# Half of the depthwise convolution's taps on VectorE instead of TensorE, in a two-layer decoder step

## The reference, cut to what matters

```python
def conformer_conv(h, buf, w_pw1, b_pw1, w_dw, b_dw, ln_g, ln_b, w_pw2):
    u = h @ w_pw1 + b_pw1
    u = u[..., :D_CONV] * jax.nn.sigmoid(u[..., D_CONV:])
    full = jnp.concatenate([buf.astype(u.dtype), u], axis=1)
    z = lax.conv_general_dilated(full, w_dw[:, None, :], (1,), 'VALID', ..., feature_group_count=D_CONV) + b_dw
    z = jax.nn.silu(layernorm(z, ln_g, ln_b))
    return z @ w_pw2, full[:, -(CONV_WIDTH - 1):]
```

## Time and profile before

| | us |
|---|---|
| median of 3 runs | 823.9 |
| lowest and highest | 823.81, 825.25 |
| the profiled execution's own time | 823.19 |
| its span, first to last instruction | 821.6 |
| TensorE busy | 749.0 (91%) |
| VectorE busy | 322.2 (39%) |
| ScalarE busy | 208.4 (25%) |
| mean granted TensorE clock | 0.968 |

### The profile page before, as it was taken

The page is one execution under the profiler, slowest core; times in us unless marked ns, Lnnn a source line. Parts: engine busy times, 40 slices in busy tenths (PEclk is TensorE's granted clock), DMA queues, the critical chain, the costliest instruction groups (busy, mean ns, idle before and its releaser), DMA issues.

```text
span 821.6 us, 16618 instructions
## 1 busy us (share of the span) xinstructions
PE 749.0 (91%) x6420; PEld 532.6 (65%) x6420; DVE 322.2 (39%) x952; ACT 208.4 (25%) x498; POOL 59.0 (7%) x101
## 2 busy tenths in 40 slices
PE   8999999999979879889999898999999798788894
PEld 6877577766646446648876456777766465456483
DVE  3434343523323131334556656243233231313445
ACT  2100242521212111123225543143311111111232
POOL 1600200000000000000052620000000000000000
PEclk9999999999999898999999999999999899989998
DMA  9873896799999999999358774994999999999901
GB/s 358 301 257 85 246 420 250 277 407 424 421 418 424 421 419 422 414 412 397 138 191 300 242 208 177 421 408 173 419 419 421 420 420 420 421 419 416 375 2 53
DMA packets 65346, 271.83 MB, mean 331 GB/s; under 512 B 8032, under 2 KB 19504, under 8 KB 45296
## 3 DMA queue, kind: packets, MB, share of 16 engines
q1 hardware_dynamic: 58320, 260.30, 79.7%
q10 hardware_dynamic: 4048, 5.84, 2.3%
q0 software_dynamic: 2896, 4.58, 1.9%
HBM read 262.44 MB, written 3.61 MB: 324 GB/s over the span
## 4 chain that ended last, share of the span: by engine, by line
PE 52%; DMA 20%; SPq 5%; DVE 2%; ACT 2%; issue 2%; DVEq 0%; ACTq 0%
PE bank L630 17%; DMA ring<-in_moe_w_up 11%; PE bank L772 11%; PE bank L746 7%; DMA arena<-in_moe_w_up 6%; PE bank L801 4%; SPq L2236 3%; PE bank L815 3%; DMA ring<-in_moe_w_down 2%; DMA arena<-in_moe_w_down 2%; PE bank L1105 1%; PE bank L707 1%; PE bank L940 1%; SPq L2226 1%; PE bank L1130 1%
## 5 line engine op out<-in xcount | busy, mean ns | idle before, releaser
L772 PE MATMUL bank<-ring,arena 128*32 128x256 f32 x1344 | 115.5, 411 | 13.7 <-DMA ring<-in_moe_w_up 10.3
L630 PE MATMUL bank<-xn_sq,ring 128*128 128x264 f32 x480 | 108.6, 387 | 1.1 <-issue 0.6
L746 PEld LDWEIGHTS bank<-arena 128*128 128x128 f32 x864 | 99.0, 192 | 9.2 <-issue 9.1
L630 PE MATMUL bank<-arena,ring 128*128 128x264 f32 (+1 forms) x440 | 103.0, 389 | 0.1
L746 PE MATMUL bank<-arena 128*128 128x128 f32 (+1 forms) x864 | 102.6, 277 | 0.5 <-DVE arena L1419 0.5
L630 PEld LDWEIGHTS bank<-xn_sq,ring 128*128 128x128 f32 x480 | 90.8, 190 | 18.5 <-issue 2.3
L1451 DVE TENSOR_TENSOR arena<-arena,bank 128x128 f32<-128x128 f32 x34 | 9.8, 287 | 220.0 <-ACT arena L1900 220.0
L772 PEld LDWEIGHTS bank<-ring,arena 128*32 128x32 f32 x1344 | 61.4, 118 | 52.9 <-issue 30.2
L630 PEld LDWEIGHTS bank<-arena,ring 128*128 128x128 f32 x440 | 81.9, 190 | 18.3 <-issue 3.8
L772 PE MATMUL bank<-xn_sq,arena 128*32 128x256 f32 x384 | 52.9, 437 | 21.7 <-DMA ring<-in_moe_w_up 21.7
L1469 DVE TENSOR_TENSOR hT<-hT,bank 128x264 f32<-128x264 f32 x144 | 61.5, 428 | 20.6 <-PE bank L826 11.8
(11 more groups left out here) (278 smaller groups left out, 868.9 us busy)
## 6 DMA issues: line engine op xcount, KB each, us to landing
ring<-in_stream SPq DMA_DIRECT2D x34, 1024.0 KB, 12.6
ring<-in_moe_w_gate SPq DMA_DIRECT2D x34, 1024.0 KB, 19.3
ring<-in_moe_w_up SPq DMA_DIRECT2D x34, 1024.0 KB, 21.4
ring<-in_moe_w_down SPq DMA_DIRECT2D x28, 1024.0 KB, 21.9
arena<-in_moe_w_down SPq DMA_DIRECT2D x24, 1024.0 KB, 22.1
arena<-in_moe_w_gate SPq DMA_DIRECT2D x14, 1024.0 KB, 19.0
arena<-in_moe_w_up SPq DMA_DIRECT2D x14, 1024.0 KB, 21.1
xn_sq<-in_moe_w_gate SPq DMA_DIRECT2D x12, 1024.0 KB, 18.8
```

The source lines that it names most:

```text
L630: t = mm(ps[:, 0:cols], lhs(k), rhs(k), start=(k == 0), stop=(k == n - 1))
L746: t = mm(bank[k // 4][:, (k % 4) * n:(k % 4 + 1) * n], XR[:, i, k * P:(k + 1) * P], S[:, j % 2, i, 0:n], start=(i == 0), stop=(i == 2))
L772: t = mm(bank[2 + r][p0:p0 + U, 0:F].rearrange("p (c f) -> p c f", c=2), x, w[i][:, :, k * F + c * P:k * F + (c + 1) * P], start=(k == 0), ...
```

## The change

Chunks 0 to 3 (two pairs, `PD = 2`, `CD = 4`) leave TensorE's taps. VectorE computes them as 31 accumulating instructions for each chunk, 124 in all, on 128 partitions by 256 tokens, straight from `uT` at offset j. Two chunks alternate. Each instruction waits for the end of the one two before it (`s_tap`). From chunk 2 on, four of them stand between line 1263 and the wait for the sigmoid, and nine behind the gating: 13 in each of six chunks, 78 in all; the last 46 stand behind the loop. TensorE does only `taps(2)` and `taps(3)`, both behind `expand(7)`; `taps(0)` between `expand(4)` and `expand(5)` is gone. The copies for pairs 0 and 1 and half of the diagonals are gone too, the waits of pairs 2 and 3 for a free buffer with them. The tap weights `wdw` and `wq` move to another place of the arena, and `dg` is half as large.

```diff
+PD = 2
+CD = 2 * PD
+NTAPS = CD * CW
+TAPS_WAITING, TAPS_EACH = 4, 13
...
-            if p == 0:
+            if p == PD:
                 eng.wait_ge(s_zero, 2)
-            if p >= 2:
+            if p >= PD + 2:
                 arrive(eng, ("taps", 2 * (p - 2) + 1))
...
             for c in range(KD):
                 expand(c)
-                if c == 4:
-                    taps(0)
-            for p in range(1, PAIRS):
+            for p in range(PD, PAIRS):
                 taps(p)
...
                 v.tensor_tensor(sgu[:, c % 4, :], ps[:, 0:T], rstd[:], ALU.mult).then_inc(is_free(key), 1)
+                if c >= 2:
+                    vector_taps((c - 2) * TAPS_EACH, TAPS_WAITING)
                 dve.wait_ge(s_sgu, c + 1)
...
+            def vector_taps(start, n):
+
+                for i in range(start, min(start + n, NTAPS)):
+                    c, j = 2 * (i // (2 * CW)) + i % 2, i % (2 * CW) // 2
+                    src = uT[:, c, j:j + TP]
+                    if j == 0:
+                        dve.wait_ge(s_glu, c + 1)
+                        v.tensor_scalar(zT[:, c, 0:TP], src, tap[:, c, 0:1], vcol("conv_b_dw", c), ALU.mult, ALU.add)\
+                         .then_inc(s_tap, 1)
+                    else:
+                        dve.wait_ge(s_tap, i - 1)
+                        v.scalar_tensor_tensor(out=zT[:, c, 0:TP], in0=src, scalar=tap[:, c, j:j + 1],
+                                               in1=zT[:, c, 0:TP], op0=ALU.mult, op1=ALU.add).then_inc(s_tap, 1)
...
             for c in range(KD):
                 glu(c)
-                if c == 4:
-                    prompt_taps(0)
-                    prompt_taps(1)
-                    add_chunk(1)
+                if c >= 2:
+                    vector_taps((c - 2) * TAPS_EACH + TAPS_WAITING, TAPS_EACH - TAPS_WAITING)
...
-            for c in range(2, KD):
+            vector_taps((KD - 2) * TAPS_EACH, NTAPS)
+            dve.wait_ge(s_tap, NTAPS)
+            for c in range(1, CD):
+                add_chunk(c)
+            for c in range(CD, KD):
                 prompt_taps(c)
...
-                if c and c % 2 == 0:
+                if c > CD and c % 2 == 0:
                     shift(c // 2 - 1)
...
-            for c in range(KD):
-                g.tensor_tensor(dg[:, c], wq[:, c * NQ * TQ:(c + 1) * NQ * TQ].unsqueeze(2)
+            for c in range(CD, KD):
+                g.tensor_tensor(dg[:, c - CD], wq[:, c * NQ * TQ:(c + 1) * NQ * TQ].unsqueeze(2)
...
             for p in range(PAIRS):
-                shift_blocks(sp, "sp", p)
+                if p >= PD:
+                    shift_blocks(sp, "sp", p)
```

More of the change, by code:

```diff
@@ L270, in build @@
         mu, q = place(q, T)
-        dg, q = place(q, KD, NQ * TQ, CG)
+        wdw, q = place(q, CW * KD)
+        wq, q = place(q, KD * NQ * TQ)
+        dg, q = place(q, KD - CD, NQ * TQ, CG)
         shifted = []
@@ L275, in build @@
             shifted.append(u4)
-        wdw, q = place(q, CW * KD)
-        wq, q = place(q, KD * NQ * TQ)
         assert q <= ARENA, q
@@ L411, in build @@
         s_dve = sem("dve_steps")
-        s_pl = sem("pool_steps")
+        s_tap = sem("taps_on_vector")
         s_zc = sem("centred_chunks")
@@ L536, in copied @@
         def copied(eng, p):
-            eng.wait_ge(s_u4[p % 2], sum(by_queue(x) for x in range(p % 2, p + 1, 2)))
+            eng.wait_ge(s_u4[p % 2], sum(by_queue(x) for x in range(p % 2, p + 1, 2) if x >= PD))
             if copies("pool", p):
@@ L656, in taps @@
                     ps = open_bank(pe, ("taps", c))
-                    pe.wait_ge(s_dg, c + 1)
+                    pe.wait_ge(s_dg, c - CD + 1)
                     for q in range(TQ):
                         for b in range(NQ):
-                            t = mm(ps[CG * b:CG * (b + 1), 0:TP], dg[:, c, TQ * b + q, :],
+                            t = mm(ps[CG * b:CG * (b + 1), 0:TP], dg[:, c - CD, TQ * b + q, :],
                                    shifted[p % 2][:, b, c % 2, NQ * q:NQ * q + TP], start=(q == 0), stop=(q == TQ - 1))
@@ L1282, in add_chunk @@
             def add_chunk(k):
-                freed(dve, ("taps", k))
+                if k >= CD:
+                    freed(dve, ("taps", k))
                 if k > 1:
@@ L2106, in _ @@
             pool.dma_start(spill[:, 0:PIN_EARLY], early_pins).then_inc(s_spill[0], 16)
[L2107 to L2112, removed]
             def moe(l):
```

## The result

The changed kernel takes 829.02 us (the median of 20 executions, 824.26 to 833.82), the kernel before beside it on the same chip 822.86 us (20 executions, 819.25 to 830.1). The ratio is 1.0070, 95% interval 1.0053 to 1.0088: slower by some 6 us. The forecast was 831.3 us in a range of 826.5 to 842.

What follows compares the result with a forecast made beforehand. TensorE was taken to set the pace until 96 us, VectorE's taps after the change: 6.1 us later there plus 1.3 us of clock, +7.4 on 823.19, 830.6; with 0.7 for the median 831.3, range 826.5 to 842.

Steps and rivals of the forecast that it cites:

- Who sets the end: End of the tap stage: VectorE's taps finish last, and TensorE, done at 88.1 us, waits 14 us for them.
- The sum for VectorE: VectorE's gating, sample taps and 124 taps end at 98.1 us; after additions the last bias line starts 6.1 us later.
- The diagonals: GpSimd's diagonals beside VectorE's first gatings: with four instead of eight, gating runs clean and chunk 2 starts 2.6 us earlier.
- TensorE's taps: TensorE's conv taps: two pairs fewer save 14.2 us; after 6.6 us idle the last pair ends at 88.1.
- The clock: TensorE's two sums after its 14 us wait run at a lower clock: 0.9 plus 0.4, 1.3 us in all.
- Passed on one to one: Behind the stage everything keeps its order, so the delay of 6.1 + 1.3 = 7.4 us reaches the total.
- No overlap: Rival on VectorE's taps: each waits for the one before, 0.48 us each, +9.9 us, 841.2; chance 0.10.
- Cheap taps: Rival on VectorE's taps: 0.345 us each, like a tensor_tensor, VectorE ends 6.8 us earlier, 824.5; chance 0.06.
- a faster kernel: Rival on VectorE's taps: distance under 0.327 us gives a gain; at 0.30 the time is 819; chance 0.04.
- Swallowed later: Rival behind the stage: the weight stream swallows the delay, 824 us; chance 0.04.
- Starved copies: Rival on GpSimd's five copies of the last pair: starved beside VectorE's stream, +16 us, 840; chance 0.03.

Runs made afterwards that it cites:

- without the tail: The changed kernel with the last 46 of 124 taps not done; total of 1394.49 us says nothing, first subtraction at 91.48 us.
- with dearer taps: The changed kernel with taps chunk by chunk, each waiting for the one directly before; 840.86 us, ratio 1.0234.
- with another place for TensorE's wait: The changed kernel with eleven instead of 13 taps between gatings, so twelve taps move behind the loop; 829.01 us, ratio 1.0093.
- four extra diagonals: The changed kernel with GpSimd building four more unused diagonals ahead of the four needed; 833.97 us, ratio 1.0140.
- the repeat: The changed kernel timed again with no edit; 828.78 us, ratio 1.0089; its profiled execution took 823.42 us.
- with one pair: The changed kernel with PD = 1: VectorE keeps two chunks (62 taps), TensorE three pairs; 815.58 us, ratio 0.9917.
- the late wait: The changed kernel with VectorE's wait for tap weights and conv state moved to the first instruction touching the state; 827.19 us, ratio 1.0049.
- with idle products: Three kernels: the changed kernel plus unused TensorE products, 25 calls behind taps(3), or 12 ahead of it and 25 or 31 behind; ratios 1.0015, 1.0061, 1.0130.
- with three chunks: The changed kernel with chunk 3's taps back on TensorE (VectorE keeps 93) and the later state wait; 813.55 us, ratio 0.9883.
- the kernel with 25 calls of idle products: The changed kernel with 25 calls of unused TensorE products behind taps(3), ahead of the sum over channels; 824.58 us, ratio 1.0015.
- the kernel with the short filling: The kernel with three chunks on VectorE, plus the state's transfer issued by SP and four calls of idle products; 814.98 us, ratio 0.9904.

## Why the prediction was right

The forecast held in its sign, its range and its mechanism; its +7.4 us was a little high against some 6. The steps on the stage are shown one by one; what happens behind `w_pw2` agrees over medians only.

| step | forecast | profile after |
|---|---|---|
| distance of two taps | 0.40 | 0.396 |
| chunk 2 starts | 33.8 | 33.61 |
| last tap ends | 98.1 | 97.1 |
| TensorE's wait ahead of the last pair | 6.6 | 5.59 |
| TensorE's last pair ends | 88.1 | 88.6 |
| TensorE's wait for VectorE | 14 | 12.61 |
| last bias line, later by | 6.1 | 5.0 |
| clock, until the first subtraction | 0.9 | 1.07 |
| clock, sum of squares | 0.4 | 0 |
| `w_pw2`, later by | 7.4 | 6.05 |

- **Who sets the end.** Right, and shown from both sides: without the tail the stage is 12.35 us shorter, with dearer taps 14.4 us longer, with another place for TensorE's wait the same within 0.8 us.
- **The sum for VectorE.** It was 1.1 us too large. The last tap ends 1.0 earlier: 0.2 from the earlier start of chunk 2, 0.004 x 124 = 0.5 from the distance, and 0.3 from the four tensor_scalars, which start 0.32 apart ((0.73 - 0.41) in the row of line 1288) and were priced at 0.40. The chain of additions behind was right: 101.00 - 97.1 = 3.9 us, forecast 4.0.
- **The diagonals.** Right: 1.07 became 0.49, and four extra diagonals bring it back.
- **TensorE's taps.** Its last pair took 9.05 us and not 7.11, since the clock was down behind the 5.59 us of waiting already (0.65 granted over 80 to 85 us). The forecast hadn't priced that; it cost nothing, 12.61 us of waiting lie behind it.
- **The clock.** Right in size for the two sums, 1.07 us. The sum of squares took 3.80 us, as in the earlier trace rows, in this execution; in the repeat it took 4.34. So 1.1 to 1.6 in all for the changed kernel, with 1.3 forecast. In its variants without idle products it was between 3.80 (each tap waits, behind 18.94 us of waiting) and 4.70 (four diagonals more), so the length of the wait alone does not set this term. The forecast of 0.4 was an estimate between the 0 and 0.54 seen in the changed kernel, and that the whole came so near is in part luck.
- **Passed on one to one.** Right until `w_pw2`, and over the medians. The start of `w_pw2` in the profile and the median, both against the kernel before, moved by +6.05 and +6.2 us in the changed kernel, -5.5 and -5.8 with one pair, +20.5 and +18.8 where each tap waits, +7.7 and +7.6 with eleven taps, +8.6 and +7.4 in the repeat, +5.7 and +5.1 with the late wait, +10.1 and +10.9 with four diagonals more. In the other five it misses by 3 to 5 us: +5.6 and +2.5, +8.7 and +5.0, +6.0 and +11.4 with idle products, -3.6 and -8.5, -5.2 and -8.1 with three chunks. So for a single kernel, an agreement to 0.2 us is in part luck. In the changed kernel's profiled execution 1.5 us of the delay are given back by `s_perm`: before, the router's 24 transposes ran at a low clock (line 707 in 4.50 us), after, they ran at full clock (line 709 in 2.84) and a low stretch came behind them. In the repeat the transposes took 2.84 us too, and line 568 behind them 1.94 in place of 3.62. Where such a stretch falls shifts between kernels and between executions, and the forecast had no term for it. The DMA queues are dry ahead of the stream in the changed kernel too; its window beside those of the earlier trace rows:

```profile
140.00:144.00 4.00, 4.00 (x18) 2.99 (x18) 1.25 (x4) 0.24 (x1) 0.00 (x0) 1.00 0.00 0
```

- **The rivals.** No overlap: what the taps cost if each needs the one before, 0.521. Cheap taps at 0.345, and the still cheaper ones of a faster kernel: false, the distance is 0.396. Swallowed later: false over the medians; but a single execution can give much of it back (the repeat's profile is 8.6 us late at `w_pw2`, and its own time 2.0 above the median before). Starved copies: false; GpSimd's timeline of the kernel after has all five issues in 2.72 us beside nine taps of VectorE (72.80 to 76.44).

```profile
73.20 2.72 POOL L554 DMA_DIRECT2D arena<-arena  x5 [47.42 <-DVE arena L1271]
```

What stays open is why the kernel with 25 calls of idle products is some 3 us faster than its stage explains (4.5 us in the ratio, 1.0 in the stage, with an interval of 2.5 us either way), why the two kernels with three chunks gain 3 to 5 us more than theirs, and what makes the "issue" stalls long or short. Ratios of kernels that differ in TensorE's instructions carry an uncertainty of some us that no interval of the runs shows.

## What to carry to other kernels

When work moves from one engine to another, write down both engines' chains to the point where they meet: this change took 14.2 us from TensorE's and put 49 us of taps on VectorE's. VectorE's last bias line came 12 us behind the end of TensorE's shortened chain (101.00 against 88.6), so it had room for some 37 us of taps, an estimate from these rows. With half the move (62 taps) or three quarters (93) the same idea is 0.8 to 1.2% faster instead of 0.7% slower. A chain that becomes the longest brings its own first link along: VectorE's begins at a transfer whose landing TensorE's chain had covered before, and the scatter of that landing is now in the stage. In accumulating chains interleave two of them: the distance of two steps falls from 0.521 to 0.396 us.

## What was unexpected in the hardware

- Idle products kept the clock up where they reached nearly to the next real work: with 0.60 and 0.65 us of idle behind them line 681 took 0.68 us, with 3.00 us behind them 1.22. The length of the idle time alone does not tell: behind 3.29 us in the kernel with three chunks the same two matmuls took 0.68, and the clock fell only behind them. A pair of taps behind 2.42 us took 7.11 us there, and 8.80 behind 2.45 us in the kernel with the short filling.
- An "issue" stall of TensorE at one source line took 0, 1.2 to 1.7, or 3.6 to 3.75 us in kernels that differ only far ahead of it, and 0 and 1.49 us in two executions of one kernel.
- VectorE's 0.23 us for eight columns became 1.88 us beside a diagonal, so a tiny instruction can pay the price of a large one.
